# Decays of a gated linear attention in four pieces instead of eight, two of their steps on another engine, and eight small weight loads through another queue

## The reference

```python
log_gate = lambda lr, j: jax.nn.log_sigmoid(lr @ gate_up[j] + gate_bias[j]) / GLA_TAU   # 4 heads x 256, j = 0, 1
```

## Time and profile before

| | |
|---|---|
| median of 3 runs | 2344.84 us (2344.71 to 2346.23) |
| profiled execution | 2347.94 us, its span 2345.8 us |
| busy in the span: TensorE / VectorE / ScalarE / GpSimd | 2319.1 / 1611.8 / 1202.2 / 68.3 us |
| mean granted TensorE clock | 0.997 |
| transferred | 420.33 MB, mean 179 GB/s |

### The profile page before, as it was taken

One profiled execution on the slowest core, in us unless ns is written; L12 is line 12 of the kernel. 1 busy time (PEld: TensorE's weight loads), 2 busy tenths in 40 slices (PEclk: granted clock), 3 DMA queues, 4 the chain that ended last, 5 costly groups with the idle time before them and its releaser, 6 DMA issues.

```text
span 2345.8 us, 50450 instructions
## 1 busy us (share of the span) xinstructions
PE 2319.1 (99%) x19290; PEld 2269.8 (97%) x19290; DVE 1611.8 (69%) x2321; ACT 1202.2 (51%) x1639; POOL 68.3 (3%) x119
## 2 busy tenths in 40 slices
PE   8999999999999999999999899999999999999999
PEld 7999999999999999999998899999999999999998
DVE  6667676777755775677574667776877567767775
ACT  5546455554434444444478554555554445444543
POOL 1000010000000000000020011000000000000000
PEclk9999999999999999999999999999999999999999
DMA  6555565565565565656565544555655665566665
GB/s 196 162 150 157 166 170 150 172 197 179 184 204 185 181 195 187 193 179 201 186 176 158 145 117 126 148 184 182 200 193 189 214 195 190 186 212 189 201 198 170
DMA packets 431890, 420.33 MB, mean 179 GB/s; under 512 B 26163, under 2 KB 430941, under 8 KB 431741
## 3 DMA queue, kind: packets, MB, share of 16 engines
q1 hardware_dynamic: 417680, 415.16, 57.0%
q10 hardware_dynamic: 14076, 3.30, 1.1%
HBM read 416.31 MB, written 2.10 MB: 178 GB/s over the span
## 4 chain that ended last, share of the span: by engine, by line
PE 93%; DVE 3%; ACT 3%; issue 1%; DMA 0%; ACTq 0%; DVEq 0%
PE ps L1662 29%; PE ps L1660 26%; PE ps L1661 25%; PE ps L1658 6%; PE ps L1909 1%; DVE w_lo L1120 1%; PE ps L1903 1%; ACT w_hi L611 1%; PE ps L1931 1%; PE ps L1697 0%; ACT L1001 0%; PE ps L1863 0%; PE ps L1739 0%; PE ps L1741 0%; PE ps L1740 0%
## 5 line engine op out<-in xcount | busy, mean ns | idle before, releaser
L1660 PE MATMUL ps<-act_hi,w_hi 128*128 128x272 f32 (+1 forms) x4864 | 1366.5, 281 | 9.2 <-DVE w_lo L1120 9.2
L1661 PE MATMUL ps<-act_lo,w_hi 128*128 128x272 f32 (+1 forms) x4864 | 1352.0, 278 | 0.0
L1662 PE MATMUL ps<-act_hi,w_lo 128*128 128x272 f32 (+1 forms) x4864 | 1351.9, 278 | 0.0
L1120 DVE TENSOR_TENSOR w_lo<-raw,w_hi 128x1024 fp32r<-128x1024 f32 (+1 forms) x800 | 951.1, 1208 | 487.4 <-ACT w_hi L611 454.5
L611 ACT ACTIVATE w_hi<-raw 128x1024 fp32r<-128x1024 f32 (+1 forms) x796 | 813.2, 1034 | 629.6 <-PE ps L1662 605.7
L1660 PEld LDWEIGHTS ps<-act_hi,w_hi 128*128 128x128 f32 x4864 | 926.6, 190 | 15.2 <-DVE w_lo L1120 6.9
L1661 PEld LDWEIGHTS ps<-act_lo,w_hi 128*128 128x128 f32 x4864 | 926.7, 191 | 1.2
L1662 PEld LDWEIGHTS ps<-act_hi,w_lo 128*128 128x128 f32 x4864 | 926.3, 190 | 0.0
L1662 PE MATMUL ps<-g_both,w_lo 128*128 128x272 f32 (+1 forms) x1408 | 388.4, 276 | 0.0
L1662 PEld LDWEIGHTS ps<-g_both,w_lo 128*128 128x128 f32 x1408 | 268.2, 190 | 0.0
L1658 PE MATMUL ps<-g_both,w_hi 128*128 128x512 f32 x676 | 222.2, 383 | 0.0
(11 more groups left out here) (300 smaller groups left out, 1183.2 us busy)
## 6 DMA issues: line engine op xcount, KB each, us to landing
raw<-in_ffn_w_up SPq DMA_DIRECT2D x352, 512.0 KB, 4.6
raw<-in_ffn_w_down SPq DMA_DIRECT2D x128, 512.0 KB, 4.1
raw<-in_ab_w_in SPq DMA_DIRECT2D x96, 512.0 KB, 3.8
raw<-in_c_w_in SPq DMA_DIRECT2D x96, 512.0 KB, 3.8
raw<-in_ffn_w_down SPq DMA_DIRECT2D x64, 384.0 KB, 3.8
raw<-in_ab_w_out SPq DMA_DIRECT2D x32, 512.0 KB, 3.4
raw<-in_c_w_out SPq DMA_DIRECT2D x32, 512.0 KB, 4.4
tok<-in_x SPq DMA_DIRECT2D x8, 256.0 KB, 6.9
```

The lines of the kernel that those rows point to most:

```text
L1120: V.tensor_tensor(w_lo[:, s % 4, 0:kc * 256], raw[:, s % 4, 0:kc * 256], w_hi[:, s % 4, 0:kc * 256].bitcast(F32), ALU.subtract).then_inc(S ...
L1660: mm(o, wh, moving(xh, kk), start=(c == 0 and k == 0), stop=False)
L1661: mm(o, wh, moving(xl, kk), start=False, stop=False)
L1662: ins = mm(o, wl, moving(xh, kk), start=False, stop=end)
```

## The change

The decays are made in four pieces, one for each head and both directions (4 tiles), each over 6 chunks. TensorE does four matmuls for a piece, into four banks. The bias is added by VectorE, which also writes -|x| into `ge` (the smaller of -x and x), with a new semaphore `gu_neg`; ScalarE is left with Exp, Ln and the decay's Exp, each over 4 tiles at once. `ge` is twice as large. The eight loads of the convolutions' parameters are issued by SP, four after the fetch of chunk 6 and four after that of chunk 7. VectorE's memset of `tail_st` moves behind the others.

```diff
-        ge = sb("ge", [P, 2, T], at=zone + 40 * TB)
+        ge = sb("ge", [P, 2, 2, T], at=zone + 40 * TB)
...
             for s in range(4, 8):
                 fetch(gemms[0], 0, s)
+                if s >= 6:
+                    for m in range(4 * (s - 6), 4 * (s - 5)):
+                        layer, tap = m // 4, m % 4
+                        v = ffn_conv_w[layer, tap] if tap < 3 else ffn_conv_b[layer]
+                        sp.dma_start(stage[0:2 * FT, m, :], v.rearrange("(m p) -> m p", p=P)).then_inc(S("conv_in"), 16)
...
-            def load_conv(m):
-                layer, tap = m // 4, m % 4
-                v = ffn_conv_w[layer, tap] if tap < 3 else ffn_conv_b[layer]
-                act.dma_start(stage[0:2 * FT, m, :], v.rearrange("(m p) -> m p", p=P)).then_inc(S("conv_in"), 16)
...
-                elif q < 4:
-                    for m in range(3 * q - 3, min(3 * q, 8)):
-                        load_conv(m)
-                else:
+                elif q == 4:
                     load_tail(c_w_in[0], C_COLS, LRS, GATES, "c_tail_in")
...
             def decays():
-                def decay_of(q):
-                    act.wait_ge(S("gu_min"), q + 1)
-                    b2 = bc[:, q % 2, 2 * (q // 2):2 * (q // 2) + 2, :]
+                def decay_of(p):
+                    act.wait_ge(S("gu_min"), p + 1)
+                    b2 = bc[:, :, 2 * p:2 * p + 2, :]
                     A(b2, b2, ACT.Exp, scale=1.0 / GLA_TAU).then_inc(S("b_done"), 1)
-                for q in range(8):
-                    j, k = q % 2, 2 * (q // 2)
-                    yield
-                    act.wait_ge(S("gu_mm"), q + 1)
-                    if q:
-                        act.wait_ge(S("gu_min"), q)
-                    for m in range(2):
-                        n = 8 * j + k + m
-                        ins = A(bc[:, j, k + m, :], pm[2 * (q % 2) + m][:, 0:T], ACT.Identity, bias=vec[:, V_GB + n:V_GB + n + 1])
-                    ins.then_inc(S("gu_x"), 1)
-                    act.wait_ge(S("gu_x"), q + 1)
-                    chain.link(A(ge[:, :, :], bc[:, j, k:k + 2, :], ACT.Abs))
-                    yield
-                    chain.link(A(ge[:, :, :], ge[:, :, :], ACT.Exp, scale=-1.0))
-                    if q:
-                        decay_of(q - 1)
-                    A(ge[:, :, :], ge[:, :, :], ACT.Ln, bias=1.0).then_inc(S("gu_ln"), 1)
-                    yield
-                decay_of(7)
+                for p in range(GLA_HEADS):
+                    yield
+                    yield
+                    act.wait_ge(S("gu_neg"), p + 1)
+                    chain.link(A(ge[:, :, :, :], ge[:, :, :, :], ACT.Exp))
+                    if p:
+                        decay_of(p - 1)
+                    yield
+                    A(ge[:, :, :, :], ge[:, :, :, :], ACT.Ln, bias=1.0).then_inc(S("gu_ln"), 1)
+                    yield
+                    yield
+                    if p == GLA_HEADS - 1:
+                        decay_of(p)
+                    yield
...
             def decays():
-                yield
-                for q in range(8):
-                    j, k = q % 2, 2 * (q // 2)
-                    yield
-                    yield
-                    dve.wait_ge(S("gu_ln"), q + 1)
-                    b2 = bc[:, j, k:k + 2, :]
-                    V.scalar_tensor_tensor(b2, b2, 0.0, ge[:, :, :], ALU.min, ALU.subtract).then_inc(S("gu_min"), 1)
+                for p in range(GLA_HEADS):
+                    b2 = bc[:, :, 2 * p:2 * p + 2, :]
+                    yield
+                    dve.wait_ge(S("gu_mm"), p + 1)
+                    for j in range(2):
+                        for m in range(2):
+                            n = 8 * j + 2 * p + m
+                            ins = V.tensor_scalar(bc[:, j, 2 * p + m, :], pm[2 * j + m][:, 0:T], vec[:, V_GB + n:V_GB + n + 1], None, ALU.add)
+                    ins.then_inc(S("gu_x"), 1)
+                    dve.wait_ge(S("gu_x"), p + 1)
+                    if p:
+                        dve.wait_ge(S("gu_min"), p)
+                    V.scalar_tensor_tensor(ge[:, :, :, :], b2, -1.0, b2, ALU.mult, ALU.min).then_inc(S("gu_neg"), 1)
+                    yield
+                    yield
+                    yield
+                    dve.wait_ge(S("gu_ln"), p + 1)
+                    V.scalar_tensor_tensor(b2, b2, 0.0, ge[:, :, :, :], ALU.min, ALU.subtract).then_inc(S("gu_min"), 1)
+                    yield
                     yield
...
-                        dve.wait_ge(S("b_done"), 2 * hd + 2)
+                        dve.wait_ge(S("b_done"), hd + 1)
...
-                for q in range(8):
-                    j, k = q % 2, 2 * (q // 2)
-                    if q >= 2:
-                        pe.wait_ge(S("gu_x"), q - 1)
-                    for m in range(2):
-                        ins = mm(pm[2 * (q % 2) + m][:, 0:T], gup_r[:, j, (k + m) * P:(k + m + 1) * P], tail_r[:, :], start=True, stop=True)
+                for p in range(GLA_HEADS):
+                    if p:
+                        pe.wait_ge(S("gu_x"), p)
+                    for j in range(2):
+                        for m in range(2):
+                            c = (2 * p + m) * P
+                            ins = mm(pm[2 * j + m][:, 0:T], gup_r[:, j, c:c + P], tail_r[:, :], start=True, stop=True)
                     ins.then_inc(S("gu_mm"), 1)
-                    yield
-                    yield
-                    yield
+                    for t in range(6):
+                        yield
```

More of the change, by code:

```diff
@@ L272, in build @@
             ml_ptdone ml_ptcopied ml_pv ml_stored ml_normed ml_made po_sq po_sum po_ss po_rt po_gate
-            gu_mm gu_x gu_ln gu_min b_done gl_kc gl_km gl_up gl_g gl_cp gl_pv gl_stored
+            gu_mm gu_x gu_neg gu_ln gu_min b_done gl_kc gl_km gl_up gl_g gl_cp gl_pv gl_stored
             lmask_done out_done out_evac out_sent sel_done""".split()
@@ L1109, in _ @@
             V.memset(tail[:, :], 0.0)
-            V.memset(tail_st[:, :, GATES:LRS].bitcast(F32), 0.0)
             V.memset(eps[:, 0:1], EPS)
@@ L1114, in _ @@
             dve.sem_inc(S("bank_free"), 2)
+            V.memset(tail_st[:, :, GATES:LRS].bitcast(F32), 0.0)
             def lo(g, it, s):
@@ L1913, in gla @@
                 pe.wait_ge(S("bank_free"), 2 + G["v_in"]["gr0"])
-                pe.wait_ge(S("gu_x"), 8)
+                pe.wait_ge(S("gu_x"), GLA_HEADS)
                 for t in range(GL_TICKS):
```

## The result

The changed kernel takes 2327.68 us (median of 4 runs, 2326.25 to 2328.46), the kernel before beside it 2345.53 us (4 runs, 2344.71 to 2348.24). The ratio is 0.9921, with an interval from 0.9904 to 0.9938: faster by 0.8%, 17.9 us. The forecast was 2326.9 and -17.9. The profiled execution took 2327.98 with a span of 2326.3.

What follows compares the result with a forecast made beforehand. TensorE was taken to bound the kernel except in the decay stretch, where ScalarE set the pace. 14.0 + 1.6 + 0.7 + 1.6 = 17.9 us off 2344.84 gave 2326.9; forecast range 2324 to 2331, 8 in 10 within 2323 to 2334.

Steps and rivals of the forecast that it cites:

- The bound and the 14.0 us: Decay stretch beside `q_in` and `k_in`: ScalarE sets the pace; at TensorE's pace 82.0 us become 68.0, saving 14.0.
- No drain behind the loads: ScalarE's table loads in the decays: 1283 ns each, without the Trainium skill's some 1380 ns of drain.
- The wait at the end and the clock behind it, -1.6: End of the decay stretch: TensorE's 5.0 us wait for `k_in`'s store goes, so the low clock after it goes: -1.6 us.
- Start, -0.7: Chunk 5 at the start: without ScalarE's inline loads `w_lo` starts 0.7 us earlier, VectorE's own order being late next.
- Start, clock, -1.6: After chunk 5 at the start: with shorter TensorE gaps the low clock doesn't come, -1.6 us, the less certain term.
- Slack of 2.4 us per head: Hand-over chain between ScalarE and VectorE in each head: smallest slack before a `w_lo` is late, 2.4 us.
- Rival A: Decay heads: ScalarE and VectorE partly bind, the hand-over being longer than laid out; 8 us come back, 2335; chance 0.09.
- the upper price: VectorE's bias addition out of PSUM: at most 0.72 us each, 0.48 assumed; slack would then be 1.4 us.
- Rival D: Decay heads: hand-over doesn't overlap the chunks, +61 instead of -14, 2402; decides from 6.9 us beyond the chain; chance 0.03.
- B: Linear attention: the time comes back there as TensorE meets `step` and `take` on VectorE; 2335; chance 0.07.
- C: Whole kernel: the waits move and nothing is gained, 2345; chance 0.04.
- E: Start: the change there does nothing or the clock stays low, 2328.5 to 2329.2; chance 0.72 together with the forecast.

Runs made afterwards that it cites:

- eight-piece kernel: Changed kernel with eight decay pieces of 544 columns instead of four, bias and -|x| still on VectorE, new start kept: 2335.04 us, ratio 0.9945.
- merging alone: Changed kernel with bias and absolute value back on ScalarE, still four pieces of 1088 columns: 2329.55 us, ratio 0.9921.
- the decays alone: Changed kernel with the eight convolution loads back on ScalarE and the `tail_st` memset where it was: 2329.58 us, ratio 0.992.
- the square moved first: Changed kernel with ScalarE's fourth Square ahead of its issues of gate_b and tail_w: 2329.66 us, ratio 0.992; with VectorE's last sums also one chunk later: 2327.78 us.
- the kernel with seven memsets: Changed kernel with seven GpSimd memsets per head between VectorE's negation and ScalarE's Exp, 6.9 us longer hand-over: 2354.84 us, ratio 1.0032.
- The kernel with two memsets: Changed kernel with two GpSimd memsets per head between VectorE's negation and ScalarE's Exp, hand-over some 2.1 us longer: 2333.48 us, ratio 0.9937.

## Why the prediction was right, point by point

**The bound and the 14.0 us.** Right and shown: either half of the decays' change alone brings TensorE back to its pace. 68.0 us were forecast from TensorE's pace, 68.11 or 68.12 measured in five executions (four kernels with this form of the decays), with ScalarE 48.3 busy (forecast some 50), the decay groups 16.6 to 17.2 us apart, and no wait.

**No drain behind the loads.** Right: the groups behind the loads of line 990 idle 0.0 us, the loads of line 986 begin 0.1 us in all behind what stands before them, and the chain kept its times. The Trainium skill, "ScalarE: Activation LUTs", section "What ACT_TABLE_LOAD costs", adds some 1380 ns of drain to each switch; its load of 1283 ns agrees with both profiles, the drain shows in neither, nor at the end of the eight-piece kernel (load at 1283.75, Ln at 1285.05).

**The wait at the end and the clock behind it, -1.6.** Right: measured 1.3 to 1.6 (1043.9 or 1043.67 to 1042.33). The kernel with eight pieces on VectorE shows the pair apart from the rest: it keeps the pace, but has the wait (3.71) and the low clock. Most of the wait goes because the last Ln stands two chunks before the end; the last 1.6 us go because the copies no longer stand before Exp (merging alone keeps them). What was not foreseen is how narrowly: 0.47 us.

**Start, -0.7.** Right, 0.67 (0.80 between the kernel with the decays alone and the changed one), and VectorE's order is next, as laid out.

**Start, clock, -1.6, "the less certain term".** The size of one fall is right, its certainty not. It varies from execution to execution: in the kernel before it came in the first profile and not in the second, with the same gaps. It varies with the kernel as well: all nine timed runs of the changed kernel have 1.000, and with the loads on SP and the old decays none of ten has under 0.998, while 11 of 13 of the kernel before have. With the square moved first, six of ten runs have 0.999 again. And a second place at 80 us, not in the prediction, costs as much. When both come, they make 3.2 us, and when neither comes the term is nothing. So the agreement of -17.9 with 17.9 is partly luck. Without either place, 13.9 + 1.6 + 0.7 = 16.2 us are left, and the four runs of the kernel before at 0.999 (2343.2 to 2344.3) lie some 16 above the changed kernel (2327.7 to 2328.4, on another chip). And on the last chip, where eight of the nine runs of the kernel before had 0.996 to 0.998, its median was 2348.3 beside 2328.03, a gain of 20.3.

**Slack of 2.4 us per head.** Mis-sized, in two ways. It holds for a head that starts rested and isn't the last. The last one has 0.47 us before its store is late; the chain was laid out for the `w_lo` of each chunk and not for that store. And over four heads in a row 2.1 us already cost 5.3 us in all, because a late `w_lo` delays the fetch into the same buffer and hands the delay to the next head. Rival A would have begun much nearer than written, though the additions, at 492 ns and not the upper price of 0.72 us, stayed clear of it: at the upper price, some 0.9 us later, the last store would have been some 0.4 us late (an estimate from these two numbers).

**Rival D, its price.** Beyond the slack each us was counted once. The waits of 3.6 to 3.9 us brought the low clock too, 2.9 us per head, so the kernel became slower than before at a hand-over 6.9 us longer, where the prediction put the break-even; by its own rule, 4.5 x 4 = 18 us against 17.9, it would have been even, and it was 0.3% slower. B did not come: nothing in the linear attention waits more than before. C is out. E is out by the profile, which has the 0.67 us, and not by the median: 2327.68 lies between the forecast and E. The range written for E, 2328.5 to 2329.2, doesn't follow from its own 0.7 to 2.3 us either; 2326.9 + 0.7 is 2327.6.

Open: what decides in one execution whether the clock falls at 35 and at 80 us, and why the kernels differ in how often. No experiment here turned it on or off at will.

## What to carry to other kernels

When two engines feed a third, find which of them waits for the third and which never does: the idle column before the groups said it (0.3 us of idle for ScalarE, 44.7 for VectorE), while the busy time of TensorE said 99%. Work of fixed cost per piece is saved by fewer pieces, and once the pace is TensorE's again, moving part of it to another engine too is worth only what the end of the stretch still waits for: either half alone gave 9.2 or 12.3 of 13.9 us here, so they don't add. Price a wait of TensorE with the clock behind it. Lay a chain out to the very last result that the next stage needs, not only round by round, and a slack over several rounds with the buffers in between.

## What the runs showed of the hardware

- In the profiled executions the granted clock fell during or behind each of the waits of 3.6 to 5.0 us after the start (four in the kernel with seven memsets, 3.71 with VectorE's share alone, and 5.01 in three executions), behind waits of 2.06 or 2.07 three times in four, and never behind single waits of 1.0 to 1.6 us. The kernel with two memsets, one of the three, has a mean clock of 1.000 in its three other timed runs. Behind the pair of 0.91 and 1.14 to 1.27 us at 35 us it fell in two executions of three, behind 0.91 and 0.47 in none.
- It also fell without a gap: at 77 to 80.5 or at 79 to 84 us, in three of twelve profiled executions (two of kernels whose small loads stood on ScalarE, one with them on SP), right behind 24 matmuls of four columns each (the gates of the mLSTM). In others the same instructions left it at 1.00. One such fall costs 1.6 us.
- Three small transfers took 1.96 us to issue on ScalarE. With six of them before it, its next copy began 2.17 us behind the end of the Square; with them on SP it began at once (1.11 us from 30.07 on for the Square, the copy at 31.09). On SP the eight cost nothing that shows.
